# Down products of the feed-forward stages as pairs of half-row products on two accumulators

## What is computed

```python
def swiglu(x, w_gate_up, w_down):          # D_MODEL 1024, D_FF 2816
    gu = x @ w_gate_up
    gate, up = gu[..., :D_FF], gu[..., D_FF:]
    return (jax.nn.silu(gate) * up) @ w_down
...
x = layer_norm(DN_ALPHA * x + swiglu(x, w_gate_up[i], w_down[i]), ln_g[i, 1], ln_b[i, 1])
```

## Time and profile before

| what | value |
|---|---|
| median of 3 runs | 2470.38 us (2468.71 to 2470.68) |
| the profiled execution's own time | 2470.61 us |
| its span, first to last instruction | 2468.8 us |
| TensorE products busy | 2400.2 us, 97%, 13024 products |
| TensorE weight loads busy | 1990.6 us, 81% |
| VectorE, ScalarE, GpSimd busy | 61%, 47%, 4% |
| DMA | 419 MB, mean 170 GB/s |

### The profile page before, as it was taken

The page is one execution under the profiler, slowest core; times in us unless marked ns, Lnnn a source line. Parts: engine busy times, 40 slices in busy tenths (PEclk is TensorE's granted clock), DMA queues, the critical chain, the costliest instruction groups (busy, mean ns, idle before and its releaser), DMA issues.

```text
span 2468.8 us, 32201 instructions
## 1 busy us (share of the span) xinstructions
PE 2400.2 (97%) x13024; PEld 1990.6 (81%) x13024; DVE 1511.0 (61%) x2130; ACT 1171.0 (47%) x1609; POOL 107.9 (4%) x138
## 2 busy tenths in 40 slices
PE   6999999999999999999999999999999999999999
PEld 5788887877888778886888878887888878987887
DVE  6754655456546475467655676676555676677553
ACT  3644355455443564436434355573434455564442
POOL 2100000001000010000100100000100000000000
PEclk9999999999999999999999999999999999999999
DMA  6355343343553445543654335353754434445642
GB/s 234 137 205 204 137 176 132 137 171 128 199 202 137 174 149 207 205 157 121 249 195 167 119 137 205 120 205 128 273 197 161 146 109 178 146 173 180 234 172 85
DMA packets 263122, 419.00 MB, mean 170 GB/s; under 512 B 12192, under 2 KB 149408, under 8 KB 262976
## 3 DMA queue, kind: packets, MB, share of 16 engines
q1 hardware_dynamic: 258112, 400.15, 45.8%
q0 software_dynamic: 4864, 16.80, 1.9%
HBM read 415.86 MB, written 1.05 MB: 169 GB/s over the span
## 4 chain that ended last, share of the span: by engine, by line
PE 87%; DVE 6%; ACT 3%; issue 2%; DMA 1%; POOL 1%; SPq 0%; DVEq 0%; ACTq 0%; POOLq 0%
PE bank_L L1979 39%; PE bank_L L1963 18%; PE bank_S L2183 7%; PE bank_O L2183 7%; PE bank_L L1960 3%; PE bank_O L2121 2%; DVE wlo L1270 2%; PE bank_T L2104 1%; PE bank_T L2166 1%; PE bank_S L1963 1%; PE bank_S L2092 1%; ACT whi L969 1%; PE bank_O L1963 1%; PE bank_T L1920 1%; PE bank_T L1992 1%
## 5 line engine op out<-in xcount | busy, mean ns | idle before, releaser
L1270 DVE TENSOR_TENSOR wlo<-raw,whi 128x2048 fp32r<-128x2048 f32 (+1 forms) x332 | 712.3, 2170 | 286.7 <-ACT whi L969 286.2
L969 ACT ACTIVATE whi<-raw 128x2048 fp32r<-128x2048 f32 (+1 forms) x332 | 593.8, 1817 | 61.0 <-DMA raw<-in_w_in 21.2
L1979 PE MATMUL bank_L<-whi,xt_hi 128*128 128x512 f32 x1440 | 572.1, 397 | 9.2 <-DVE wlo L1270 7.5
L1979 PE MATMUL bank_L<-wlo,xt_hi 128*128 128x512 f32 x1440 | 564.3, 392 | 0.0
L1979 PE MATMUL bank_L<-whi,xt_lo 128*128 128x512 f32 x1440 | 563.4, 391 | 0.0
L1979 PEld LDWEIGHTS bank_L<-whi,xt_hi 128*128 128x128 f32 x1440 | 272.0, 189 | 64.8 <-issue 8.6
L1151 ACT ACTIVATE tok<-bank_L 128x256 f32<-128x256 f32 x132 | 50.7, 384 | 566.3 <-PE bank_L L1979 566.3
L1979 PEld LDWEIGHTS bank_L<-wlo,xt_hi 128*128 128x128 f32 x1440 | 271.6, 189 | 57.6
L1963 PE MATMUL bank_L<-whi,xt_hi 128*128 128x512 f32 (+1 forms) x800 | 314.5, 393 | 2.9 <-DVE wlo L1270 2.9
L1979 PEld LDWEIGHTS bank_L<-whi,xt_lo 128*128 128x128 f32 x1440 | 272.2, 189 | 53.7
L1963 PE MATMUL bank_L<-wlo,xt_hi 128*128 128x512 f32 (+1 forms) x800 | 308.7, 386 | 0.0
(11 more groups left out here) (309 smaller groups left out, 3141.8 us busy)
## 6 DMA issues: line engine op xcount, KB each, us to landing
raw<-in_w_gate_up SPq DMA_DIRECT2D x176, 512.0 KB, 5.7
raw<-in_w_in SPq DMA_DIRECT2D x72, 1024.0 KB, 6.3
draw<-in_w_down SPq DMA_DIRECT2D x44, 1024.0 KB, 6.2
raw<-in_ffn_w_up SPq DMA_DIRECT2D x88, 512.0 KB, 5.7
raw<-in_b_w_qkv SPq DMA_DIRECT2D x36, 1024.0 KB, 7.0
draw<-in_ffn_w_down SPq DMA_DIRECT2D x22, 1024.0 KB, 5.7
raw<-in_w_lift SPq DMA_DIRECT2D x32, 512.0 KB, 4.4
raw<-in_a_w_qkv SPq DMA_DIRECT2D x12, 1024.0 KB, 8.1
```

The costliest lines, as they stand in the source:

```text
L969: act.activation(wide(whi, w, nkc, ncols)[:, ks, :], wide(raw, w, nkc, ncols)[:, ks, :], ACT.Copy) \
L1270: dve.tensor_tensor(wide(wlo, w, nkc, ncols)[:, ks, :], wide(raw, w, nkc, ncols)[:, ks, :], wide(whi, w, nkc, ncols)[:, ks, :].bitcast(F32 ...
L1979: mm = pe.matmul(banks[bank][:, :], xx[:, k, t * P:(t + 1) * P], ww[:, k, :], start=(k == 0 and q == 0), stop=(k == KC - 1 and q == 2))
```

## The change

In the loop, `down(j - 1, 0)` and `down(j - 1, 1)` become one call of a new function, `down_in_halves(j - 1)`. Each 128-row product is done as two of 64 rows, on rows 0 to 63 and on rows 64 to 127. A chunk has four groups q. In a group the lower half goes to the accumulator `order[q]` and the upper half to `order[(q + 2) % 4]`, so that the two of a pair write different banks; with `order` = (0,0), (0,1), (1,0), (1,1) the groups pair banks S0 with O0, S1 with O1, O0 with S0, O1 with S1. A group runs over k = 0, 1 and the three terms: six pairs. An accumulator is therefore written by both halves, in groups q and q + 2, and a new semaphore, `half_done`, which TensorE itself counts and waits for, keeps them in order: group 2 waits for group 0 of the chunk, group 3 for group 1, group 0 for group 2 of the chunk before, group 1 for group 3 of the chunk before (its last product counts `down_done`). Both halves of the chunk's split weights are waited for at the start.

```diff
--- before.py
+++ after.py
@@ -180,6 +180,7 @@
         draw_full = [sem("draw_full0"), sem("draw_full1")]
         dhi_done, dlo_done = sem("dhi_done"), sem("dlo_done")
         down_done = sem("down_done")
+        half_done = sem("half_rows_done")
         sum_done = sem("sum_done")
         silu_done, h_done = sem("silu_done"), sem("hidden_done")
         tp_done = sem("transposed")
@@ -1994,6 +1995,7 @@
                 held[name] = (tlo_done, st["at"]["sg"] + g + 1)
 
             ALL, LATE = list(range(KC)), 6
+            in_halves = [0]
 
             for st in stages:
                 at = st["at"]
@@ -2201,12 +2203,35 @@
                     up(1, 1, ALL[KC // 2:])
                     down(0, 0)
                     down(0, 1)
+                    def down_in_halves(j):
+
+
+                        d, b, done = d0 + j, j % 2, in_halves[0]
+                        pe.wait_ge(tlo_done, sg0 + j + 1)
+                        pe.wait_ge(dlo_done, 2 * d + 2)
+                        order = [(t, h) for t in range(T) for h in range(2)]
+                        for q in range(4):
+                            before = done + (-1, 0, 2, 4)[q]
+                            if before > 0:
+                                pe.wait_ge(half_done, before)
+                            if q == 1:
+                                pe.wait_ge(down_done, d)
+                            for k in range(2):
+                                for yy, ww in ((yt_hi, dhi[d % 2, k]), (yt_lo, dhi[d % 2, k]), (yt_hi, dlo[:, d % 2, k, :])):
+                                    two = []
+                                    for half, (t, h) in enumerate((order[q], order[(q + 2) % 4])):
+                                        rows = slice(half * HD, (half + 1) * HD)
+                                        two.append(pe.matmul(banks[ACC[t][h]][:, :], yy[rows, 2 * b + k, t * P:(t + 1) * P],
+                                                             ww[rows, h * NW:(h + 1) * NW], start=False, stop=False))
+                            two[0].then_inc(half_done, 1)
+                            two[1].then_inc(half_done if q < 3 else down_done, 1)
+                        in_halves[0] += 7
+
                     for j in range(2, FJ - 1):
                         up(j, 0)
                         turned_hidden(j - 1)
                         up(j, 1)
-                        down(j - 1, 0)
-                        down(j - 1, 1)
+                        down_in_halves(j - 1)
                     turned_hidden(FJ - 2)
                     up(FJ - 1, 0)
                     down(FJ - 2, 0)
```

## The result

The changed kernel takes 2492.86 us (median of 3 runs, 2490.22 to 2492.97) against 2470.38: ratio 1.0089, 95% interval 1.0067 to 1.0112, 22.5 us slower. The forecast was 2489.6 in a range of 2474 to 2499. The profiled execution took 2492.97 us, its span 2491.2.

The account below looks back on a forecast made before the run. TensorE's stream was taken to bound the kernel. Only the 48 round trips counted, +19.2 us on the profiled 2470.61 (2489.8), or 2489.6 on the runs' median, with pair steps, waits and issue at 0; range 2474 to 2499.

Parts of the forecast that it names:

- The bound: Six feed-forward stretches: TensorE busy throughout, so a nanosecond added to its stream is a nanosecond of the span.
- The round trip: Between up and down and back, once per chunk: full to half rows and back costs 0.40 us, 48 times, +19.2 us.
- What the switch waits for: At a change of row form, the first load waits for the running product's end, the first product for its load.
- The pair step: Down's 1152 pair steps: each takes 0.227 us like a full-row product, change 0; bounds -15.0 to +8.1 us.
- Rival B: Down's pairs lose the fp32r excess, steps of 0.214 to 0.216 us: +4.2 to +6.5 in all, 2475 to 2477; chance 0.28.
- Waits, increments, issue: Down chunks on TensorE: met waits, eight semaphore increments instead of one, and issuing more instructions each cost 0.
- Rival C: Waits on TensorE's own semaphore stop early weight loads at three places per chunk: +19.2 + 14.4, 2504 us; chance 0.09.
- D: Down's fp32r halves run one after the other, not side by side: +19.2 + 261.5, 2751 us; chance 0.05.
- E: Faster: pair steps at 0.216 us and a cheaper switch behind 512-column products, 2462 us; chance 0.06.
- What would show it: Trace signs in a stage: chunk cadence 16.80 to 17.20 us, switch gaps 0.31 to 0.34, stage middle 3.2 us longer.

Follow-up runs that it names:

- own_wait: Kernel before, with one wait after each of the 48 loop chunks for the chunk's own last product, full rows only: 2484.02 us, ratio 1.0063.
- full_waits: Changed kernel with full-row products in place of the pairs, keeping all its waits and eight increments per chunk: 2470.11 us, ratio 1.0001.
- one_by_one: Changed kernel with each group's six lower half-row products first, then its six upper ones: 2520.09 us (one run).

## Why the prediction was right, and what it missed

- **The bound.** Right: TensorE stayed busy for the whole of the stretches, and what was added to its stream there, 23.0 us by the stage time, came out in the time, 22.5.
- **The round trip.** 0.40 us in the sum, read from two places in attention with plain fp32. The four gaps were 0.40 together (0.32, 0.33, 0.32, 0.34 against four of 0.227), so the row carried over to fp32r with 512 columns. The mis-sized part is that these were only the gaps: the rows ended with the second product after the return, and the ten longer steps behind each restart (0.04 to 0.05 each time) stood outside them. The round trip measures 0.49 in the cadence and 0.48 over all stages (23.0/48). The sum's 19.2 us was 3.8 short of that; the forecast was only 3.3 short, since the rest of the program took a little less. Part of the longer steps could have been read before, right behind the round trip that the sum was priced from:

```profile
1459.82 0.39 PE L1963 MATMUL bank_L<-wlo,xt_hi 128*128 128x512 f32 x1
```

1458.90 The earlier trace rows to 1459.82 are four steps, 0.92 to 0.93 us where four of 0.227 are 0.91. That is 0.02, and the steps are back at 0.227 after it: half of what one restart in the changed kernel shows, so reading on would have brought the sum nearer and not all the way.
- **What the switch waits for.** The prediction says that the first load of the other row form waits for the running product's end. The gaps don't show that. The load and its product start 0.32 us after the product ahead, which stands 0.39 by the profile's modelled end; where TensorE was made to wait for its product's end (own_wait), the distance was 0.45. So the switch costs less than a wait for the end by semaphore, and what it waits for stays open.
- **The pair step.** 0.227 forecast, 0.227 measured. The nearest rows, plain fp32, had no difference between full and half rows, and fp32r has none either. Rival B, at 0.214 to 0.216, didn't occur. The Trainium skill, "TensorE: Matmul & The Clock Gate", section "Back-to-back issue gap", gives 512/2.4 + 2.5 ns as the gap of isolated warm products; no run here has it for fp32r, at either number of rows, and the trace's 227 ns decides.
- **Waits, increments, issue.** 0 forecast. 0 shown by full_waits for the waits and increments. The 26.3 ns per increment of "The cost: per-tile semaphore tail" in the same page of the Trainium skill does not show where nothing waits for the tail: eight increments a chunk left the time at 1.0001.
- **Rival C** (own waits stop the early loads): no. **D** (halves one after the other): no, they start 0.00 to 0.01 apart. **E** (the switch cheaper behind 512 columns of fp32r): no, 0.32 as in attention.
- **What would show it** named a cadence of 17.20 and gaps of 0.31 to 0.34; the gaps were right, the cadence was 17.29. A stage's middle was to grow by 3.2 us and grew by 3.6.
- **The range.** 2474 to 2499 held rival B as well as the forecast, so the time alone would have proved little. It is the steps in the trace that tell the forecast from B.

## What to carry to other kernels

Going from products of one row form to products of the other interrupts TensorE's stream. Here a round trip cost 0.43 us with one pair in it and 0.49 with 12, 24 or 48 pairs, about two products of 512 columns. A pair of half-row products cost what one full-row product costs, and a half-row product without a partner cost the same. So in place of full rows the pairs gained nothing and paid for the round trips. Where the contraction has 64 rows anyway, these prices say that pairs should take half the steps of lone products, and that few long pieces are better than many short ones; no kernel here tried it with fp32r. When a stop is priced from a trace, measure until the steps are back at their pace and not to the first products after it.

## What the runs showed that I had not expected

Half-row products need not be neighbours in the program to run side by side: in one_by_one an upper product started ahead of three lower ones that come before it in the program, and from there each half of the array took its own products at its own pace, 0.01 us apart at first and 0.11 one step later. And after the return from 24 pairs and after a plain wait alike, the stream of 512-column fp32r products ran ten steps of about 0.231 to 0.233 before it was back at 0.227, all at granted clock 1.00. Behind one pair, and behind the transposes at 654.19, there were five such steps.
